# Split weights of a feed-forward product: one 512-column product for the high weights in place of two of 258 columns, from tile four (the fifth) on

## What is computed

```
u = rms_norm_2(x, g_ffn[l]) * (1 + sc_f) + sh_f
h = jax.nn.silu(u @ w_ffn_gate[l]) * (u @ w_ffn_up[l])
x = x + gt_f * (h @ w_ffn_down[l])
```

## Time and profile before

| | us |
|---|---|
| runs | 1960.17, 1960.33, 1960.48 |
| median | 1960.33 |
| span of the profiled execution (first to last instruction) | 1958.4 |
| PE busy | 1938.1 (99%) |
| DVE busy | 1495.5 (76%) |
| ACT busy | 1142.0 (58%) |
| POOL busy | 233.8 (12%) |
| products of f_hi and f_lo (3 groups of 704) | 199.9 + 199.0 + 198.9 |

### The profile page before, as it was taken

How to read it: one execution, slowest core, us unless ns; L and a number is a source line. 1 busy time by engine, 2 the same in 40 slices (tenths; PEclk the granted TensorE clock), 3 DMA queues, 4 the chain that set the end, 5 groups by cost and what they waited for, 6 DMA issues and landing times.

```text
span 1958.4 us, 39766 instructions
## 1 busy us (share of the span) xinstructions
PE 1938.1 (99%) x13232; PEld 1788.5 (91%) x13232; DVE 1495.5 (76%) x3643; ACT 1142.0 (58%) x2377; POOL 233.8 (12%) x262
## 2 busy tenths in 40 slices
PE   9999999999999999999999999999999999999998
PEld 8779999999888899999989899999999989999997
DVE  6757798888778878888876477888886567787765
ACT  5544666998444444444466566654457566765454
POOL 1000596565000000000000000010000000010000
PEclk9999999999999999999999999999999999999999
DMA  8536555444775687777765533566665553355552
GB/s 305 184 107 221 200 173 171 145 140 141 252 258 192 203 307 284 281 287 289 252 220 184 183 113 115 171 230 254 247 226 174 189 166 108 124 179 183 185 189 97
DMA packets 109455, 388.23 MB, mean 198 GB/s; under 512 B 12160, under 2 KB 16528, under 8 KB 108304
## 3 DMA queue, kind: packets, MB, share of 16 engines
q1 hardware_dynamic: 95040, 335.40, 50.0%
q10 hardware_dynamic: 8096, 28.70, 4.2%
q0 software_dynamic: 6192, 22.55, 3.1%
HBM read 379.76 MB, written 6.82 MB: 197 GB/s over the span
## 4 chain that ended last, share of the span: by engine, by line
PE 89%; DVE 7%; issue 1%; ACT 1%; DVEq 1%; ACTq 0%
PE bank L751 15%; PE bank L759 15%; PE bank L756 15%; PE bank L999 8%; PE bank L1002 8%; PE bank L1005 8%; PE bank L1066 3%; PE bank L896 1%; PE bank L1255 1%; PE bank L1294 1%; PE bank L1211 1%; DVE arena L2290 1%; DVE arena L2283 1%; PE bank L1160 1%; PE bank L1157 1%
## 5 line engine op out<-in xcount | busy, mean ns | idle before, releaser
L1434 ACT ACTIVATE part_hi<-ring 128x512 fp32r<-128x512 f32 x1124 | 693.5, 626 | 395.4 <-PE bank L756 223.7
L2072 DVE TENSOR_TENSOR part_lo<-ring,part_hi 128x512 fp32r<-128x512 f32 (+1 forms) x764 | 505.6, 684 | 176.7 <-ACT part_hi L1434 165.5
L751 PE MATMUL bank<-u_hi,part_hi 128*128 128x256 f32 (+1 forms) x1888 | 545.3, 289 | 4.9 <-POOL part_lo L1977 3.4
L759 PE MATMUL bank<-u_hi,part_lo 128*128 128x256 f32 (+1 forms) x1888 | 529.7, 281 | 0.0
L756 PE MATMUL bank<-u_lo,part_hi 128*128 128x256 f32 x1808 | 505.9, 280 | 0.0
L751 PEld LDWEIGHTS bank<-u_hi,part_hi 128*128 128x128 f32 (+1 forms) x1888 | 354.6, 188 | 14.1 <-POOL part_lo L1977 4.6
L759 PEld LDWEIGHTS bank<-u_hi,part_lo 128*128 128x128 f32 (+1 forms) x1888 | 356.7, 189 | 0.0
L756 PEld LDWEIGHTS bank<-u_lo,part_hi 128*128 128x128 f32 x1808 | 339.6, 188 | 3.1
L999 PE MATMUL bank<-part_hi,w_hi 128*128 128x512 f32 x688 | 269.4, 392 | 0.6 <-DVE w_lo L2390 0.2
L1002 PE MATMUL bank<-part_hi,w_lo 128*128 128x512 f32 x688 | 268.0, 390 | 0.0
L1005 PE MATMUL bank<-part_lo,w_hi 128*128 128x512 f32 x688 | 267.8, 389 | 0.0
(11 more groups left out here) (334 smaller groups left out, 2988.1 us busy)
## 6 DMA issues: line engine op xcount, KB each, us to landing
ring<-stream_dram SPq DMA_DIRECT2D x606, 512.0 KB, 3.4
arena<-ada_dram ACTq DMA_DIRECT2D x54, 512.0 KB, 4.6
arena<-ada_dram POOLq DMA_DIRECT2D x42, 512.0 KB, 4.4
acts_kept<-act SPq DMA_DIRECT2D x32, 128.0 KB, 3.6
arena<-acts_kept SPq DMA_DIRECT2D x4, 1024.0 KB, 5.6
xT<-x_dram SPq DMA_DIRECT2D x4, 256.0 KB, 5.4
arena<-mem_dram SPq DMA_DIRECT2D x1, 1024.0 KB, 9.1
arena<-keys_dram SPq DMA_DIRECT2D x1, 1024.0 KB, 8.8
```

The costliest lines, as they stand in the source:

```text
L751: m = pe.matmul(o, hi, u(cc), start=first, stop=False)
L759: m = pe.matmul(o, lo, u(cc), start=False, stop=last)
L1434: act.activation(part_hi[:, h % 4, 0:width], ring[:, n % RING, (h % 2) * width:(h % 2 + 1) * width], ACT.Copy).then_inc(hi_ready, 1)
L2072: v.tensor_tensor(part_lo[:, h % 4, 0:width], ring[:, n % RING, (h % 2) * width:(h % 2 + 1) * width], part_hi[:, h % 4, 0:width], ALU.subt ...
```

## The change

A second form of the input is made while tiles 0 to 3 run as before: DVE computes x times gain times inverse root for each chunk (`normed_input`, into `uT`), ACT adds the shift and writes the high part (`normed_high`), DVE the low part (`normed_low`), side by side in `n_parts[:, c, 0:2, :]`, 512 columns. From tile 4 on, gate and up take for each chunk one product of the high weights with both parts (512 columns, into a whole bank) and one of the low weights with the high part (256 columns, into its first half): two products and two weight loads in place of three. The two halves of the bank must then be added. ACT copies the second half into SBUF (`keep_other`), DVE adds the first half to it (`add_gate`, and the first instruction of `hidden_of_sum`). Silu has no bias any more, and DVE neither copies shift columns nor multiplies by the root. PE waits for all 16 chunks' parts before tile 4. The loops on PE, ACT and DVE start with tile 4; tiles 2 and 3 are written out.

```diff
+                def ffn_in_normed(k, b, before):
+
+                    for h in (2 * k, 2 * k + 1):
+                        pe.wait_ge(lo_ready, before + (h + 1))
+                        for c in range(4):
+                            cc = (h % 2) * 4 + c
+                            hi, lo = part_hi[:, h % 4, c * P:(c + 1) * P], part_lo[:, h % 4, c * P:(c + 1) * P]
+                            both = n_parts[:, cc, :, :].rearrange("p a b -> p (a b)")
+                            if cc == 0:
+                                pe.matmul(bank[b][:, :], hi, both, start=True, stop=False).then_inc(slot_begun, 1)
+                                m = pe.matmul(bank[b][:, 0:S], lo, n_parts[:, cc, 0, :], start=False, stop=False)
+                                m.then_inc(half_begun, 1)
+                                continue
+                            m = pe.matmul(bank[b][:, 0:S], lo, n_parts[:, cc, 0, :], start=False, stop=False)
+                            if c == 0:
+                                m.then_inc(half_begun, 1)
+                            m = pe.matmul(bank[b][:, :], hi, both, start=False, stop=cc == DC - 1)
+                    return m
...
-                with pe.Fori(0, (FT - 2) // 2) as it:
+                for f in (2, 3):
+                    ffn_up(f, 3 * f - 1, l * FT, before)
+                    ffn_down(f - 1, 3 * f + 1, l * FT, before)
+                pe.wait_ge(nlo_chunk, (l + 3) * DC)
+                with pe.Fori(1, (FT - 2) // 2) as it:
                     for r in (2, 3):
-                        ffn_up(r, 3 * r - 1, l * FT + it * 2, before + it * 12)
+                        ffn_up(r, 3 * r - 1, l * FT + it * 2, before + it * 12, normed=True)
                         ffn_down(r - 1, 3 * r + 1, l * FT + it * 2, before + it * 12)
...
+                def normed_high(c):
+                    act.wait_ge(p_normed, (l + 1) * DC + (c + 1))
+                    act.activation(n_parts[:, c, 0, :], uT[:, c, :], ACT.Identity, bias=vec[:, 24 + c:25 + c])\
+                        .then_inc(nhi_chunk, 1)
+
+                def keep_other(full, b, dst, f, more):
+                    act.wait_ge(full, more + (f + 1))
+                    act.activation(dst[:, f % 2, :], bank[b][:, S:2 * S], ACT.Copy).then_inc(other_kept, 1)
+
+                def silu_of_sum(f, more):
+                    act.wait_ge(gate_scaled, more + (f + 1))
+                    g = act2[:, f % 2, :]
+                    act.activation(g, g, ACT.Silu).then_inc(silu_done, 1)
+
                 silu(0, l * FT)
+                normed_high(0)
+                normed_high(1)
                 ffn_high(3)
                 ffn_high(4)
                 silu(1, l * FT)
...
+                normed_high(2)
+                ffn_high(5)
+                normed_high(3)
+                ffn_high(6)
+                ffn_high(7)
+                silu(2, l * FT)
+                normed_high(4)
+                ffn_high(8)
+                normed_high(5)
+                ffn_high(9)
+                normed_high(6)
+                ffn_high(10)
+                normed_high(7)
+                silu(3, l * FT)
+                with act.Fori(1, (FT - 2) // 2) as it:
                     for r in (2, 3):
...
+                        ffn_high(3 * r - 1, it)
+                        ffn_high(3 * r, it)
+                        keep_other(g_full, 2 * (r % 2), act2, r, l * FT + it * 2)
+                        ffn_high(3 * r + 1, it)
+                        silu_of_sum(r, l * FT + it * 2)
+                        keep_other(up_full, 1 + 2 * (r % 2), wgt2, r, l * FT + it * 2)
...
+                def add_gate(f, kept):
+                    v.wait_ge(other_kept, kept + (2 * f - 7))
+                    g = act2[:, f % 2, :]
+                    v.tensor_tensor(g, bank[2 * (f % 2)][:, 0:S], g, ALU.add).then_inc(gate_scaled, 1)
+
+                def hidden_of_sum(f, more, kept):
+                    v.wait_ge(other_kept, kept + (2 * f - 6))
+                    v.wait_ge(d_step, more + (f - 1))
+                    up = wgt2[:, f % 2, :]
+                    v.tensor_tensor(up, bank[1 + 2 * (f % 2)][:, 0:S], up, ALU.add)
+                    v.drain()
+                    v.wait_ge(silu_done, more + (f + 1))
+                    v.tensor_tensor(wgt2[:, f % 2, :], wgt2[:, f % 2, :], act2[:, f % 2, :], ALU.mult)
...
+                scale_gate(0, l * FT)
+                normed_input(0)
+                normed_input(1)
+                ffn_low(3)
+                hidden(0, l * FT)
+                normed_low(0)
+                normed_input(2)
+                ffn_low(4)
+                scale_gate(1, l * FT)
+                normed_low(1)
+                normed_input(3)
+                ffn_low(5)
+                hidden(1, l * FT)
+                normed_low(2)
+                ffn_low(6)
+                ffn_low(7)
+                scale_gate(2, l * FT)
+                normed_input(4)
+                if l == 0:
+                    last_modulation(0, 16, 0)
+                ffn_low_half(16, 0)
+                hidden(2, l * FT)
+                normed_input(5)
+                ffn_low_half(17, 0)
+                normed_low(3)
+                ffn_low(9)
+                normed_low(4)
+                normed_input(6)
+                ffn_low(10)
+                normed_low(5)
+                normed_input(7)
+                scale_gate(3, l * FT)
+                if l == 0:
+                    last_modulation(1, 16, 1)
+                ffn_low_half(22, 0)
+                normed_low(6)
+                hidden(3, l * FT)
+                normed_low(7)
+                ffn_low_half(23, 0)
...
-                        scale_gate(r, l * FT + it * 2)
+                        add_gate(r, l * (2 * (FT - 4)) + it * 4)
...
-                        hidden(r, l * FT + it * 2)
+                        hidden_of_sum(r, l * FT + it * 2, l * (2 * (FT - 4)) + it * 4)
                         ffn_low_half(6 * r + 5, it)
```

More of the change, by code:

```diff
@@ L396, in build @@
         m_lo = nc.alloc_sbuf_tensor_at("m_lo", [P, DC, S], F32R, offset=arena_at + 4 * sqk_at)
+        n_parts = nc.alloc_sbuf_tensor_at("n_parts", [P, DC, 2, S], F32R, offset=arena_at + 4 * fqk_at)
         FW = S + 2
@@ L445, in build @@
         p_sum = sem("mixed_square_sum_ready")
-        p_normed = sem("mixed_normed_chunk_ready")
+        p_normed = sem("mixed_then_ffn_normed_chunk_ready")
         psq_ready = sem("pair_squares_ready")
@@ L478, in build @@
         lo_ready = sem("low_parts_ready")
-        nhi_chunk = sem("input_then_mixed_normed_high_chunk_ready")
-        nlo_chunk = sem("input_then_mixed_normed_low_chunk_ready")
+        nhi_chunk = sem("input_then_mixed_then_ffn_normed_high_chunk_ready")
+        nlo_chunk = sem("input_then_mixed_then_ffn_normed_low_chunk_ready")
         first_loaded = [sem(f"ada_first{i}_loaded") for i in range(4)]
@@ L538, in build @@
         gate_scaled = sem("ffn_gate_scaled")
+        other_kept = sem("ffn_other_half_kept")
         g_full = sem("ffn_gate_full")
@@ L1376, in ffn_in, with ffn_up @@
                     return m
-                def ffn_up(f, k, more, before, fresh=None):
+                def ffn_in_normed(k, b, before):
[15 more added lines that the diff above has]
+                    return m
+                def ffn_up(f, k, more, before, fresh=None, normed=False):
                     if f >= 2:
                         pe.wait_ge(silu_done, more + (f - 1))
+                    if normed:
+                        ffn_in_normed(k, 2 * (f % 2), before).then_inc(g_full, 1)
+                        pe.wait_ge(h_ready, more + (f - 1))
+                        ffn_in_normed(k + 1, 1 + 2 * (f % 2), before).then_inc(up_full, 1)
+                        return
                     ffn_in(k, 2 * (f % 2), before, fresh).then_inc(g_full, 1)
@@ L1949, in _ @@
                 silu(1, l * FT)
-                if l == 0:
-                    for r in (2, 3):
[L1952 to L1959, removed]
+                normed_high(2)
[13 more added lines that the diff above has]
+                with act.Fori(1, (FT - 2) // 2) as it:
+                    for r in (2, 3):
+                        ffn_high(3 * r - 1, it)
[4 more added lines that the diff above has]
+                        keep_other(up_full, 1 + 2 * (r % 2), wgt2, r, l * FT + it * 2)
                 ffn_high(3 * FT - 1)
@@ L2791, in hidden, with normed_input, normed_low @@
                         .then_inc(h_ready, 1)
+                def normed_input(c):
+                    v.scalar_tensor_tensor(uT[:, c, :], xT[:, c, :], gm[:, 8 + c:9 + c], rstd[:, 0:S],
+                                           ALU.mult, ALU.mult).then_inc(p_normed, 1)
+                def normed_low(c):
+                    v.wait_ge(nhi_chunk, (l + 2) * DC + (c + 1))
+                    v.scalar_tensor_tensor(n_parts[:, c, 1, :], uT[:, c, :], vec[:, 24 + c:25 + c], n_parts[:, c, 0, :],
```

(13 more changed lines are left out.)

## The result

| | kernel before | changed kernel |
|---|---|---|
| median of the runs, us | 1960.25 (1959.62 to 1960.48, 4 runs) | 1986.14 (1985.43 to 1987.64, 4 runs) |
| ratio, 95% interval | 1 | 1.0135 (1.0122 to 1.0148) |
| profiled span, us | 1958.4 | 1984.6 |
| mean granted clock | 0.999 | 0.997 |

A forecast was written before the change was run, and what follows sets the result against it. PE, busy in 99% of the span, was taken to bound the kernel. -9.0 (PE) + 12.2 (loop waits) + 1.7 (ends) + 12.8 (first tiles) + 1.8 (clock) = +19.5, giving 1979.8 us, range 1973 to 1984.

The forecast's parts named there:

- PE's gain: Gate and up products: a chunk falls from 360 to 344.5 ns, 0.25 us a tile, 9.0 us over both layers.
- The loop's waits: Loop tiles: the ACT and DVE chain makes PE wait 0.36 us a tile, +12.2 us over 2 x 17 tiles.
- 0.49 to the multiply: Link of the loop's chain in DVE's hidden_of_sum: 0.49 us from its first step to the multiply.
- The layer's end: Down 21 waits for hidden 21: PE's wait 1.13 us instead of 0.26, +0.85 a layer, +1.7.
- The first tiles: Tiles 0 to 3 and the wait at tile 4: small steps on DVE and ACT cost +6.4 us a layer, +12.8.
- the door: PE's wait at tile 4 for the last normed_low, 3.56 us in each layer.
- The clock: After PE's wait at tile 4 the granted clock may fall: 1.8 us taken, bounds 0 and 3.6.
- Table loads: normed_high, an Identity between Silus on ACT, might switch tables: 0 us taken, bounds 0 and 15 us.
- Loop keeps pace: Rival: chain is 0.36 us shorter, PE bounds tiles 4 to 21, 12.2 us of waits go: 1967.6; chance 0.13.
- Faster: Rival: normed parts hide in the first tiles and the loop keeps pace: 1953.0 us; chance 0.05.
- Weight loads set PE's pace: Rival: weight loads, not columns, set PE's pace, the chunk falls to 320 ns: 1976.4 us; no separate chance given.
- Later still: Rival: clock stays low beyond the wait at tile 4, or table loads come, 8 to 15 us more: 1988 to 1995; chance 0.07.

The follow-up runs named there:

- e1: Changed kernel with the normed parts still made and awaited at tile 4, but the loop's products and steps as in the kernel before; 1976.11 us, ratio 1.0083.
- e3: Changed kernel with ACT's order altered: high 6f + 2 ahead of the gate's copy, high 6f + 4 ahead of the up product's copy; 1968.95 us, ratio 1.0046.
- e8: Changed kernel with ACT's reordered loop and small steps spread over tiles 2 to 9 (layer 0) and 2 to 5 (layer 1), new product after; 1954.34 us, ratio 0.9972.
- e4: Changed kernel with DVE's loop over tiles 4 to 21 written out, constants in place of computed values; 1981.49 us, ratio 1.0111.
- e9: Changed kernel with 14 filling products on PE ahead of its wait at tile 4; 1982.72 us, ratio 1.0117.
- e6: Changed kernel with normed input and low parts made on GpSimd, and ACT copying the high parts where it idles; 1978.06 us, ratio 1.0094.
- e5: Changed kernel with 26 filling products of 128 columns on PE ahead of its wait at tile 4; 1986.63 us, ratio 1.0136.
- e7: Changed kernel with both the normed preparation on GpSimd and ACT's high parts moved ahead of its copies; 1961.81 us, ratio 1.0011 to the kernel before.

## Why the prediction was right in its way and short in its size

- **Direction, mechanism.** Slower, by a chain of ACT and DVE that PE waits for in the loop, and by small steps in full tiles. Both were there. e1 and e3 show one each: 16.2 for the preparation, and 17.2 back when the chain is broken by an order alone.
- **PE's gain**, -9.0: somewhat less. In the loop without waits (e3, e8) a tile is 8.31, so 0.19 less and not 0.25, 6.8 us over 36 tiles. The chunk was taken from the two sizes apart, 344.5 ns; five chunks in turn in e8 take 1460.17 to 1461.90, 346 each, which is 0.02 us a tile of the 0.06. Most of the rest lies in the gate product: in e8 it takes 2.82 us (1456.31 to 1459.13) where the up product takes 2.77, and why is open. The formula that the prediction took from the Trainium skill (TensorE: Matmul & The Clock Gate, Back-to-back issue gap), where it stands for a single product by itself, would have given 0.08 us a tile, and the rows' sum was the nearer one.
- **The loop's waits**, +12.2: this is the term that failed most. Together with PE's gain the forecast was 8.61 a tile, +0.11. Measured was 8.83 and 8.70, +0.32 and +0.19. Sixteen such distances in each layer give 8.2 us, where the forecast had 3.2 for the whole loop. The step that failed is the link "0.49 to the multiply": the changed loop has 0.57 and 0.68 there. e4 shows that most of the excess is DVE's own loop: written out, the link is 0.49 and the tiles 8.66 and 8.61. I had taken the 0.49 from rows of a loop with the same kind of wait, and it did not carry over to a step with less ahead of it; the reason stays open. That the written-out loop then meets 8.61 is in part luck. The chain was 0.13 too long, of which 0.09 is Silu without its bias, and PE's last half 0.13 too short.
- **The layer's end**, +1.7: the two starts, which answer to the earlier trace rows, are 1.28 apart, so 1.05 beyond a product's 0.23, forecast 1.13, before 0.26. Two layers: +1.6. Timeline of PE, changed kernel:

```profile
1480.83 0.39 PE L1007 MATMUL bank<-part_lo,w_hi 128*128 128x512 f32 x1
1482.11 0.50 PE L1001 MATMUL bank<-part_hi,w_hi 128*128 128x512 f32 x1 [0.89 <-DVE w_lo L2876]
```

- **The first tiles**, +12.8: e1's 16.2 less the clock's 3.4 is 12.8. Each wait was laid out by adding durations, and in layer 0 of the changed kernel they can be told one by one, as the distance between two starts less one product. They are 0.53, 0.92, 0.35, 0.50, 0.22 and 0.08 against 0.53, 0.96, 0.52, 0.56, 0.27 and 0.11, and the door 3.58 (3.42 of it in the profile's column of waits) against 3.56. So each of them came out to within 0.2 us, and this part of the sum is no luck.
- **The clock**, +1.8 with bounds 0 and 3.6: it was 3.4 by the windows and 3.0 to 3.4 by e9, near the upper bound. The value between the two had no row for it. What I used for the bound, that the level holds as long as the wait did, came out: 3.4 us of wait, some 3.4 us at 0.50. But every door of these runs behind which the clock fell has the same wait, so whether the two lengths go together is not tested.
- **Table loads**, 0: right. Between the Silus no load stands, though `normed_high` is an Identity.
- **Sum.** 12.8 (first tiles) + 8.2 (loop, tiles 5 to 21) + 1.6 (ends) + 3.4 (clock) = 26.0; measured 25.9, and 26.2 between the spans. The clock's size has no part in this check, since the 12.8 is e1's 16.2 less that same 3.4. Of the 6.4 that the forecast was short, the loop has 5.0 and the clock 1.6; the ends gave 0.1 back.
- **The rivals.** "Loop keeps pace" did not come, though e3, where it does, has 1968.95 against its 1967.6. "Faster" did not come, but its condition, normed parts that hide, is what e8 builds. "Weight loads set PE's pace": no, the chunk is 346 and not 320. "Later still" named the clock as its cause and was nearest in time, for the wrong amount: the clock came back within 4 us.

## What to carry to other kernels

A new wait costs the engine that it is put on little; look at what is queued behind it in the same queue, and put the work that others wait for ahead of it. Preparation for a faster form is best spread thin over the time in which each engine idles anyway, even if the faster form starts six tiles later: here that was worth more than the earlier start. When a chain of several queues is within 5% of the pace, count the pauses of the queue's own loop too, as a distance between two steps need not carry over from the kernel before; writing the loop out tells what they cost.

## What the runs showed of the hardware

- A wait of 3.4 us was followed by the lower clock, 0.50, for 3.4 us, a loss of 1.7 us at each of the four doors of the changed kernel and e1. In the changed kernel PE had already started again when it fell, in layer 0 of e1 it had not. With filling products ahead of the door the clock stayed at 1.00, and in e6, whose longest wait of PE was 2.1 us, its mean was 0.999.
- Two DVE steps with a wait against a computed value between them were 0.57 or 0.68 apart in the changed kernel's loop and 0.49 in the loop written out; the kernel before, with such a wait too, has 0.49. Writing the loop out was worth 4.3 to 4.65 us over 36 tiles.
- A product in plain float32 of 128 columns costs 0.22 us and shows as two records (26 as 52). e5 had counted on 0.11.
- DVE and GpSimd slow each other when both read SBUF: in the means of e7, DVE's low part takes 1.26 times as long, the fused step 1.47 times, its scaling of a bank no longer. GpSimd's multiplication of 128 x 256 takes 0.74 us where DVE mostly waits (from 1295.53) and 1.18 beside two low parts (from 1297.66).
- Silu without a bias operand takes 0.42 and not 0.51 us. By the Trainium skill (ScalarE: Activation LUTs, What ACT_TABLE_LOAD costs) each operand of that kind adds about 93 ns, and the trace agrees. In the chain this was a gain of 0.09 a tile that the forecast had left out: in e4 the next copy starts 0.33 behind Silu's start, not 0.42.
